# Two tiles in halves, output products in another slot, a last product in two banks: five reorderings of a two-layer encoder

## What is computed

```python
h = rms_norm(x, pool_norm)                      # layer 0
u, gate = split(h @ w_in)                       # 2048 + 2048 features
diff = centred_window_mean(u, 2/4/8/16 by group) - u
x = x + ((diff @ w_group) * scale * silu(gate)) @ w_out

h = rms_norm(x, att_norm)                       # layer 1
q, k, v = h @ w_in (three groups, each with its own q, k, v); gate
o_g, lse_g = dilated_window_attention(rotary(norm(q_g)), rotary(norm(k_g)), v_g, dilation g)
x = x + (sum_g softmax_g(lse) * o_g * silu(gate)) @ w_out
```

## Time and profile before

| | us |
|---|---|
| median of 3 runs (1662.98 to 1664.48) | 1664.0 |
| the profiled execution, its own time | 1664.83 |
| its span in the profile | 1663.0 |
| TensorE busy | 1650.5 (99%) |
| VectorE busy | 1139.6 (69%) |
| ScalarE busy | 840.4 (51%) |
| GpSimd busy | 271.0 (16%) |

### The profile page before, as it was taken

How to read it: one execution, slowest core, us unless ns; L and a number is a source line. 1 busy time by engine, 2 the same in 40 slices (tenths; PEclk the granted TensorE clock), 3 DMA queues, 4 the chain that set the end, 5 groups by cost and what they waited for, 6 DMA issues and landing times.

```text
span 1663.0 us, 23746 instructions
## 1 busy us (share of the span) xinstructions
PE 1650.5 (99%) x8288; PEld 1402.0 (84%) x8288; DVE 1139.6 (69%) x1896; ACT 840.4 (51%) x1980; POOL 271.0 (16%) x292
## 2 busy tenths in 40 slices
PE   8999999999999999999999999999999999999999
PEld 7888888888888888888888888888888889999887
DVE  6886677787976697686868357875368346666565
ACT  6453333432431463475655245564456257886463
POOL 1000000004312110141423012230014000005440
PEclk9999999999999999999999999999999999999999
DMA  5133333484511424332332415242324656767784
GB/s 180 52 130 124 121 108 102 152 324 157 177 46 56 148 102 150 104 121 83 127 114 89 137 66 171 82 134 96 127 78 153 229 169 227 246 221 237 241 299 159
DMA packets 146134, 242.60 MB, mean 146 GB/s; under 512 B 17249, under 2 KB 55137, under 8 KB 144994
## 3 DMA queue, kind: packets, MB, share of 16 engines
q1 hardware_dynamic: 141122, 223.79, 40.2%
q10 hardware_dynamic: 4896, 17.30, 2.8%
HBM read 161.23 MB, written 79.82 MB: 145 GB/s over the span
## 4 chain that ended last, share of the span: by engine, by line
PE 81%; ACT 1%; DVE 0%; DMA 0%; issue 0%; ACTq 0%; DVEq 0%
PE pair L1215 23%; PE pair L1217 23%; PE pair L1216 23%; PE pair L1567 4%; PE pair L1539 3%; PE pair L1487 3%; PE pair L1547 2%; ACT pp L2695 1%; DMA raw<-in_pool_w_in_dram 0%; PE pair L1236 0%; ACT turn L2746 0%; ACT qT L2688 0%; DVE w L1729 0%; ACT turn L2761 0%; DVE both L2294 0%
## 5 line engine op out<-in xcount | busy, mean ns | idle before, releaser
L1215 PE MATMUL pair<-w,turnh 128*128 128x512 f32 x640 | 249.0, 389 | 0.0
L1216 PE MATMUL pair<-w,turnh 128*128 128x512 f32 x640 | 249.0, 389 | 0.0
L1217 PE MATMUL pair<-w,turnl 128*128 128x512 f32 x640 | 249.0, 389 | 0.0
L1215 PE MATMUL pair<-w,hTh 128*128 128x512 f32 x544 | 214.0, 393 | 0.0
L1217 PE MATMUL pair<-w,hTl 128*128 128x512 f32 x544 | 212.0, 390 | 0.0
L1216 PE MATMUL pair<-w,hTh 128*128 128x512 f32 x544 | 211.7, 389 | 0.0
L2663 ACT ACTIVATE both<-pair 128x512 f32<-128x512 f32 x160 | 94.0, 591 | 176.4 <-PE pair L1217 167.6
L2157 DVE TENSOR_TENSOR both<-pair,both 128x512 f32<-128x512 f32 x120 | 81.5, 687 | 111.8 <-PE pair L1217 111.4
L2674 ACT ACTIVATE dump<-both 128x128 f32<-128x128 f32 x384 | 119.4, 311 | 64.0 <-DVE both L2157 51.5
L1215 PEld LDWEIGHTS pair<-w,turnh 128*128 128x128 f32 x640 | 120.1, 188 | 25.1 <-DVE turnl L1786 0.2
L1217 PEld LDWEIGHTS pair<-w,turnl 128*128 128x128 f32 x640 | 120.1, 188 | 25.0
(11 more groups left out here) (248 smaller groups left out, 3813.1 us busy)
## 6 DMA issues: line engine op xcount, KB each, us to landing
part_spill<-both SPq DMA_DIRECT2D x160, 256.0 KB, 3.7
both<-part_spill SPq DMA_DIRECT2D x22, 1024.0 KB, 7.2
raw_z<-in_att_w_in_dram SPq DMA_DIRECT2D x20, 1024.0 KB, 5.3
raw<-in_pool_w_in_dram SPq DMA_DIRECT2D x32, 512.0 KB, 5.2
raw<-in_att_w_in_dram SPq DMA_DIRECT2D x10, 1024.0 KB, 6.1
raw_u<-in_att_w_in_dram SPq DMA_DIRECT2D x10, 1024.0 KB, 5.7
diff_spill<-ubuf SPq DMA_DIRECT2D x16, 512.0 KB, 2.7
stage<-gate_spill SPq DMA_DIRECT2D x16, 512.0 KB, 5.8
```

The source lines that it names most:

```text
L1215: nc.tensor.matmul(out, lh, rh, start=first, stop=False, skip_group_check=onto)
L1216: nc.tensor.matmul(out, lh, rl, start=False, stop=False, skip_group_check=onto)
L1217: return nc.tensor.matmul(out, ll, rh, start=False, stop=last, skip_group_check=onto)
```

## The change

Five places are reordered; no arithmetic is left out.

1. Tiles 0 and 1 go through scaling, transposes, high and low parts in halves of 512 features. The norm's row is spread from `bufG` with ones in `whole`, with a signal behind each half; the warm-up products between the transposes are gone; the first weight is split in two halves; and the copy of the spread row to `bufG` comes after the square of tile 2.
2. The four spread output products move from h = 0 to h = 2 of steps 42 to 45.
3. `take_u` moves on ScalarE from h = 0 to h = 1 up to step 34, and to h = 2 from step 35.
4. In the couples `add_quarter(n, 2)` comes behind the splits 5 and 6.
5. The last half product is made in two parts of 256 columns in two banks, each with its own addition and store.

```diff
-        SPREAD = {(42, 0): (6, 0), (43, 0): (6, 1), (44, 0): (7, 0), (45, 0): (7, 1)}
+        SPREAD = {(42, 2): (6, 0), (43, 2): (6, 1), (44, 2): (7, 0), (45, 2): (7, 1)}
...
-                for hf in range(2):
-                    sp.wait_ge(out_added, 2 * m + hf + 1)
-                    sp.dma_start(dst[:, hf, :], xb[m % 4][:, hf, :]).then_inc(out_sent[m % 4], 16)
+                for i, (hf, at) in enumerate(((0, slice(0, 512)), (1, slice(0, 256)), (1, slice(256, 512)))):
+                    sp.wait_ge(out_added, 2 * m + i + 1)
+                    sp.dma_start(dst[:, hf, at], xb[m % 4][:, hf, at]).then_inc(out_sent[m % 4], 16)
...
-            sp.dma_start(bufS[0:1, 0:D], pool_norm[0:1, :]).then_inc(nw_in, 16)
+            sp.dma_start(bufG[0:1, 0:D], pool_norm[0:1, :]).then_inc(nw_in, 16)
...
-                last = nc.tensor.matmul(pair[1][:, 512 * hf:512 * hf + 512], bufU[:, 0:P], bufS[:, 512 * hf:512 * hf + 512],
-                                        start=True, stop=True)
-            last.then_inc(row_spread_then_half, 1)
-            warm_up(3)
-            transpose_x(0, 0)
-            warm_up(3)
-            transpose_x(0, 1)
+                nc.tensor.matmul(pair[1][:, 512 * hf:512 * hf + 512], whole[:, 0, 0:P], bufG[:, 512 * hf:512 * hf + 512],
+                                 start=True, stop=True).then_inc(row_spread_then_half, 1)
+            for part in range(2):
+                for tb in range(2):
+                    pe.wait_ge(*((dve_step, tb + 3) if part == 0 else (xn_done, tb + 1)))
+                    for kd in range(HB * part, HB * part + HB):
+                        last = nc.tensor.transpose(x_pair(0, tb)[:, kd * P:kd * P + P],
+                                                   (bufU, bufS)[tb][:, kd * P:kd * P + P], ident[:, :])
+                    last.then_inc(xt_done if part else row_spread_then_half, 1)
...
                     if c == 0 and q == 0:
-                        pe.wait_ge(hlo_done, 1)
-                        pe.wait_ge(hlo_half, 1)
+                        pe.wait_ge(hlo_half, 2)
+                        pe.wait_ge(dve_step, 5)
                     elif c == 0:
                         pe.wait_ge(hlo_done, 2 * q + 2)
                     elif c == 1 and q == 0:
-                        pe.wait_ge(half_then_row_kept, 2)
-                    if q == 0:
+                        pe.wait_ge(half_then_row_kept, 3)
+                    if q == 0 and c:
                         pe.wait_ge(*lo_ready(c))
                     wh, wl = wview(unit_of[("U", 0, c)], False), wview(unit_of[("U", 0, c)], True)
                     for kd in range(KD):
                         if c == 0 and q == 0 and kd == KD // 2:
+                            pe.wait_ge(*lo_ready(0))
                             pe.wait_ge(hlo_done, 2)
...
+                if (m, hf) == (NROW - 1, 1):
+                    for part in range(2):
+                        at = slice(256 * part, 256 * part + 256)
+                        for j in range(HALF):
+                            v = 2 * (HALF + j) + 1
+                            last = three(bank(5 + part)[:, at], y_turned(m % 2, False)[:, j, :],
+                                         y_turned(m % 2, True)[:, j, :], out_w(v, False)[:, at], out_w(v, True)[:, at],
+                                         j == 0, j == HALF - 1)
+                        last.then_inc(zo_done, 1)
+                    return
...
+                                                   in1=bufG[:, :], op0=ALU.mult, op1=ALU.mult).then_inc(xn_done, 1)
+
+                def scale_half(tb, part):
+                    at = slice(512 * part, 512 * part + 512)
+                    if part == 0:
+                        dve.wait_ge(rstd_done, tb + 1)
+                    dve.wait_ge(row_spread_then_half, part + 1)
+                    return nc.vector.scalar_tensor_tensor(out=(bufU, bufS)[tb][:, at], in0=xs[:, tb, at],
+                                                          scalar=rstd[:, tb:tb + 1], in1=pair[1][:, at], op0=ALU.mult,
+                                                          op1=ALU.mult)
+
+                def split_half(part):
+                    at = slice(512 * part, 512 * part + 512)
+                    dve.wait_ge(w_hi, 1)
+                    return nc.vector.tensor_tensor(lo_view(0)[:, at], raw[:, 0, at], hi_view(0)[:, at].bitcast(F32),
+                                                   ALU.subtract)
+
+                def lows_half(tb, part):
+                    kds = slice(HB * part, HB * part + HB)
+                    dve.wait_ge(hhi_done if part else half_then_row_kept, tb + 1)
+                    nc.vector.tensor_tensor(rowsl[:, kds, P * tb:P * tb + P],
+                                            x_pair(0, tb)[:, 512 * part:512 * part + 512].rearrange(
+                                                "p (k c) -> p k c", c=P),
+                                            rowsh[:, kds, P * tb:P * tb + P].bitcast(F32),
+                                            ALU.subtract).then_inc(hlo_done if part else hlo_half, 1)
...
-                    link(nc.vector.memset(bufS[:, 0:D], 0.0))
-                    link(nc.vector.memset(bufU[:, 0:P], 1.0))
-                    dve.wait_ge(row_spread_then_half, 1)
-                    scale(0)
-                    scale(1)
-                    split_lo(0)
-                    lows(0)
-                    lows(1)
+                    link(nc.vector.memset(bufG[:, 0:D], 0.0))
+                    link(nc.vector.memset(whole[:, 0, 0:P], 1.0))
+                    scale_half(0, 0).then_inc(dve_step, 1)
+                    scale_half(1, 0).then_inc(dve_step, 1)
+                    split_half(0).then_inc(dve_step, 1)
+                    steps[0] += 3
+                    scale_half(0, 1).then_inc(xn_done, 1)
+                    scale_half(1, 1).then_inc(xn_done, 1)
+                    lows_half(0, 0)
+                    lows_half(1, 0)
+                    split_half(1).then_inc(w_lo, 1)
+                    lows_half(0, 1)
+                    lows_half(1, 1)
                     scale(2)
                     split_lo(1)
                     scale(3)
...
                     split_product(n + 1, 4)
-                    add_quarter(n, 2)
                     split_product(n + 1, 5)
                     split_product(n + 1, 6)
+                    add_quarter(n, 2)
                     first_window(n)
...
+                if (m, hf) == (NROW - 1, 1):
+                    for i in range(2):
+                        at = slice(256 * i, 256 * i + 256)
+                        dve.wait_ge(zo_done, 2 * m + 2 + i)
+                        nc.vector.tensor_tensor(part[:, at], bank(5 + i)[:, at], part[:, at],
+                                                ALU.add).then_inc(out_added, 1)
+                    return
...
-                    highs(0)
-                    highs(1)
+                    for part in range(2):
+                        for tb in range(2):
+                            act.wait_ge(*((xt_done, tb + 1) if part else (row_spread_then_half, tb + 3)))
+                            nc.scalar.activation(rowsh[:, HB * part:HB * part + HB, P * tb:P * tb + P],
+                                                 x_pair(0, tb)[:, 512 * part:512 * part + 512].rearrange(
+                                                     "p (k c) -> p k c", c=P),
+                                                 ACT.Copy).then_inc(hhi_done if part else half_then_row_kept, 1)
+                    square(2)
                     act.wait_ge(xn_done, 2)
                     nc.scalar.activation(bufG[:, :], pair[1][:, :], ACT.Copy).then_inc(half_then_row_kept, 1)
-                    square(2)
                     split_hi(1)
                     square(3)
...
-                if h == 0 and 2 <= t <= NSTEP + 1:
+                if h == (1 if t <= merge_step(0) else 2) and 2 <= t <= NSTEP + 1:
                     take_u(t - 2)
```

More of the change, by code:

```diff
@@ L1133, in _ @@
             for i in range(4):
-                sp.wait_ge(out_sent[i], 16 * (NROW // 4 + (i == 3)))
+                sp.wait_ge(out_sent[i], 16 * (NROW // 4 + (2 if i == 3 else 0)))
         @block.gpsimd
@@ L1236, in transpose_x @@
                     last = nc.tensor.transpose(x_pair(layer, tb)[:, kd * P:kd * P + P], rows, ident[:, :])
-                    if n == 1 and kd == KD // 2 - 1:
-                        last.then_inc(row_spread_then_half, 1)
                 last.then_inc(xt_done, 1)
@@ L1791, in lows @@
                     n = layer * TB + tb
-                    if n == 1:
-                        for part, (high, low) in enumerate(((half_then_row_kept, hlo_half), (hhi_done, hlo_done))):
-                            kds = slice(KD // 2 * part, KD // 2 * (part + 1))
-                            dve.wait_ge(high, 1 if part == 0 else 2)
-                            nc.vector.tensor_tensor(rowsl[:, kds, P:2 * P],
```

(20 more changed lines are left out.)

## The result

The changed kernel took a median of 1672.05 us over 6 runs against 1664.81 us for the kernel before, beside it: a ratio of 1.0045, 95% interval 1.0033 to 1.0058. It is 7.2 us slower; 1663.2 was forecast, with 0.05 for slower.

What follows compares the result with a forecast made beforehand. TensorE, busy 1650.5 of 1663.0 us, was taken as the bound. Terms -2.5 - 0.2 - 0.3 + 2.6 - 0.4 = -0.8 us on the median of 1664.0 gave 1663.2 us, range 1658.6 to 1665.6.

Steps and rivals of the forecast that it cites:

- Start: First two tiles in halves: first product at 12.3 in place of 14.83, 2.5 us gained and not given back.
- Rival D: Start gains only 0.5 us because tile 2 or a weight transfer is next; 1665.2 us, chance 0.07.
- Weight halves ahead of the addition: Couples: splits 0.60 us earlier shorten a 1.1 us stall, the later addition loses 0.4; net 0.2 us gained.
- Results copied later: 128-wide chunk: TensorE's 0.4 us wait for an exponential goes, ScalarE idles about 0.2; 0.3 us gained.
- SyncE's chain: Steps 41 to 43: store 4.7 us later, last output-weight load issued at 1589.0, landing about 1597.8 instead of 1595.7.
- Output products in the third slot: Steps 42 to 45: waits at line 1487 covered, but 4.4 us stall in step 44 for late weight; 2.6 us lost.
- The gain of 1.8 us that was forecast for a load that is never late: Steps 42 to 45: bound on the moved products' effect, 1.8 us gained if the last output-weight load is never late.
- End: Last half product in two parts: smaller last addition and store against 0.16 us more multiplication; 0.4 us gained.
- rival C: Start: without warm-ups between transposes TensorE may fall to 1.2 GHz, costing 4 us; 1667.2 us, chance 0.05.
- A: The forecast itself: the late output-weight load gives back what the start gains; 1663.2 us, chance 0.56.

Runs made afterwards that it cites:

- run with the split first: Changed kernel with the last output-weight load issued early in step 42 and VectorE splitting the first weight's second half before the first lows; 1662.19 us, ratio 0.9989.
- run with the early load: Changed kernel with SyncE issuing the last output-weight load in step 42, right behind the one before it; 1663.34 us, ratio 0.9998.
- run with the copies alone: Kernel before with only the result copies moved later; 1669.94 us, ratio 1.0034.
- run with the products alone: Kernel before with only the four output products moved to slot 2 of steps 42 to 45; 1666.31 us, ratio 1.0016.
- run with both undone: Changed kernel with the four output products and all result copies back in slot 0; 1664.44 us, ratio 1.0005.
- the four edits: Changed kernel with last output-weight load early, copies from step 41 back in slot 0, first weight's second half split earlier, tile 2 kept before third weight's split; 1661.18 us.

## Why the prediction was wrong, step by step

**Start: wrong, 2.5 us forecast, 0.05 came.** The forecast followed TensorE, VectorE and ScalarE up to tile 2's weight split and was right there within 0.2 us: first product 12.43 (12.3), tile 2 at 15.84 (15.65), split end 16.92 (16.7). The step that failed is the sentence that TensorE has no wait between there and the couples, so nothing gives it back. Before, ScalarE came to the third unit's split at 20.33 with its engine just free: the load was hidden by the other work, with no row of waiting to show it. I did not ask when the load could leave. It leaves when the first weight's buffer comes free, and in the changed order that split is the eighth of ten half operations: 12.87, where the wide one ended at 12.99. Rival D named a weight transfer as what might be next, with a chance of 0.07, and my argument against it looked at the second unit only. The run with the split first shows it: two places up in VectorE's order, the split lets the load go 1.25 us earlier (11.52 for 12.77), the product behind tile 3 starts 0.95 us ahead of the earliest of the five runs of the changed start, and the wait is gone. How much of the lead is lost hangs on how long the load takes: the run with the early load, where it took 5.9 us, kept 0.9 to 1.6 us of it against the three executions of the start before.

**Weight halves ahead of the addition: the number right, by luck.** The wait of couple 11 is gone, and two new ones of 0.16 us each, one expected, stand at the copy behind the later addition. Net 0.35 gained, 0.2 forecast. But the wait of couple 11 belongs to one execution of the kernel before. ScalarE's split of the late weight there and what TensorE waited for, and the same split in the run with the copies alone, which has the couples as before:

```profile
286.24 1.15 ACT L2374 ACTIVATE w<-raw 128x512 fp32r<-128x512 f32 x2 [5.75 <-DMA raw<-in_pool_w_in_dram]
287.92 0.50 PE L1215 MATMUL pair<-ttwo,w 128*128 128x512 f32 x1 [0.95 <-ACT both L2514]
```

```profile
285.20 1.15 ACT L2374 ACTIVATE w<-raw 128x512 fp32r<-128x512 f32 x2 [4.71 <-DMA raw<-in_pool_w_in_dram]
```

Both pairs of loads left at 278.95, within 0.01 us; one took 7.3 us to land, the other 6.3 (6.4 in the run with the products alone), and in these last two runs TensorE has no wait in the couples. From the product behind tile 3 to the first score they take 1327.4 and 1327.3 us, the kernel before 1328.4, and the nine kernels with the addition behind the splits and no fall of the clock 1328.0 to 1328.2. So the changed order loses 0.6 to 0.8 us where that load takes 6.3 us, and gains only where it takes 7.3. The step that is not right is to price a stall of one execution as if it came each time. No run undoes this part alone.

**Results copied later, steps 24 to 31: right.** The wait for an exponential is gone; 0.36 against 0.3, and 0.42 in the run with the copies alone.

**SyncE's chain: right within 1 us in every issue** (store 4.0 us later in time, 4.7 against TensorE's steps; last load 1589.15 for 1589.0, which is 0.9 late against the steps), **and wrong in the landing.** The step that failed is "it took 8.8 us to land behind a full queue, and the queue is as full now". In the kernel before SyncE waited for the values from 1582.68 to 1585.33 while the transfers went on, so the last load's issue was late against them and its own stretch short. When that wait went, the issue moved by 2.2 us and the landing by 4.9, because the whole train of transfers had started 3.95 us later; the other 0.95 us is within the spread of the column "behind first rows' load". The load early in the queue shows that the place in the train decides. The Trainium skill, DMA: Bandwidth & Descriptors, Queues, rings and completion order, says that each DMA engine takes the descriptors of a ring in their order, though transfers need not complete in the order of issue; the runs agree with the first part (7.4 us with 2.8 MB taken from ahead of it, 11.5 with them).

**Output products in the third slot: mechanism right, size wrong.** The waits at the turned rows are gone, and there is one big wait in step 44 for the probability copy behind the output weight. 2.6 us forecast, 7.86 measured. Of the 5.3 between, 2.4 are the longer idle time in step 44 (6.83 for 4.4) and 1.4 the half clock behind it, which I had not thought of there. 0.7 fall to step 43 (6.62 us, 5.94 in the run with the products alone): the first of the two loads was late too, ScalarE waited 2.77 us for it, and the forecast gave it no term. The remaining 0.8 are spread: steps 42 and 43 else gained 0.4 in place of 0.8, step 45 0.8 in place of 1.3. The gain of 1.8 us that was forecast for a load that is never late did not come either: with the four edits, where ScalarE waits for neither load, steps 42 to 46 take 33.2 us for the 33.75 before, 0.5 us gained, since the late product brings its own wait.

**End: right**, 0.40 us for 0.4. From step 47 to the end all ten runs with the changed end take 47.9 to 48.0 us and all three with the old one 48.4. The last stores, 128 KB each, took 1.7 us from issue to landing, the 256 KB ones before 2.0: the 0.3 us of the prediction.

**The clock (rival C, 0.05).** As forecast it was to fall where the warm-ups went; it never did there. The trace shows 1.00 from 3 to 24 us in the changed kernel. It shows 1.00 from 3 to 12 us in the kernel before too, so the two paces in the earlier trace rows from which the prediction took a doubling were not the clock's. The price is seen in the run with both undone: at 0.50 one multiplication of 256 columns took 0.21 us in place of 0.12. But the granted clock fell in step 44, and once at the start, behind the wait at tile 3. The Trainium skill, TensorE: Matmul & The Clock Gate, Part 4: PE-mode transpose, says that transposes don't count as activity; nothing in these runs needs it, since what stood ahead of each fall was idle time.

So the sign came out wrong by two errors of one kind: a transfer whose time was read off its row (8.8 us) or not seen at all, since other work hid it. The two misses are 2.45 and 5.3 us. Of the rivals, A had the mechanism of step 44 and D that of the start; none had the sum of both, and none the size. The end and the copies are right, and the couples' term came out by luck.

## What to carry to other kernels

When work is brought forward, list for each load behind it the instruction that frees its buffer, and put that instruction first: a load that just lands in time shows no wait before the change and takes the whole gain after it. A stall behind a transfer in one profiled execution may be missing in the next, so it is no price until a second execution shows it. The time from issue to landing behind a busy queue belongs mostly to the bytes ahead of it and not to the load; to move a landing, move the start of the train or the load's place in it. Ahead of a copy that a store waits for, count everything that SyncE has queued behind that store: here one copy of 0.6 us set the landing of a load that was issued twelve transfers behind that store's first reader.

## What the runs showed of the hardware

TensorE's granted clock fell to 0.50 behind idle times of 2.8, 3.2, 3.9, 5.0 and 6.8 us in step 44, in all five executions that idled over 1 us there. At the start five executions idled 0.7, 1.6, 1.9, 2.2 and 2.4 us at the same place, and only the one with 1.9 us was followed by the fall, which cost it 1.5 us. So a stall can cost about 1.5 us more than its idle time, but not each time. The third weight unit's load took 5.9 to 7.6 us from issue to the split in executions of the same start, and with it the product behind tile 3 moves by up to 1.9 us from one execution to the next (0.2 of it an earlier issue). A pair of weight loads in couple 11 took 6.3, 6.4 and 7.3 us from issue to the split in three executions of the same order. Behind a full queue the same 512 KB load took 8.9 to 12.5 us from its issue, and at most 7.4 with 2.8 MB less ahead of it.
